# Scores on half-row operands, values with high and low parts side by side, and an earlier copy of the values' difference, in a windowed-attention layer

## The reference, cut to what matters

```python
def sliding_window_attention(u, wqkv, gq, gk, sinks, wo):
    ...
    q = rmsnorm(q, gq)
    k = rmsnorm(k, gk)
    ...
    scores = jnp.einsum('bnqkgd,bnskd->bnkgqs', qb, kb).astype(jnp.float32) * (HD ** -0.5)
    ...
    scores = scores - slopes[:, :, None, None] * dist.astype(jnp.float32)
    scores = jnp.where(mask[None, :, None, None], scores, -jnp.inf)
    sink = sinks.astype(jnp.float32).reshape(KV, G)[:, :, None]
    m = jnp.maximum(scores.max(axis=-1), sink)
    e = jnp.exp(scores - m[..., None])
    probs = e / (e.sum(axis=-1) + jnp.exp(sink - m))[..., None]
    o = jnp.einsum('bnkgqs,bnskd->bnqkgd', probs.astype(v.dtype), vb)
    return o.reshape(b, s, H * HD) @ wo
```

## Time and profile before

| | us |
|---|---|
| median of 3 runs | 1116.42 (1115.62 to 1116.71) |
| profiled execution | 1118.16 |
| its span | 1116.4 |
| the two attention stages and what lies around them | about 0 to 300 |
| MLP and embedding | about 300 to 1116 |

### The profile page before, as it was taken

One profiled execution on the slowest core, in us unless ns is written; L12 is line 12 of the kernel. 1 busy time (PEld: TensorE's weight loads), 2 busy tenths in 40 slices (PEclk: granted clock), 3 DMA queues, 4 the chain that ended last, 5 costly groups with the idle time before them and its releaser, 6 DMA issues.

```text
span 1116.4 us, 14894 instructions
## 1 busy us (share of the span) xinstructions
PE 1089.0 (98%) x5272; PEld 913.1 (82%) x5272; DVE 735.2 (66%) x1130; ACT 428.2 (38%) x776; POOL 148.9 (13%) x272
## 2 busy tenths in 40 slices
PE   7899999998999999999999999999999999999998
PEld 5788888887888888888888888888888888888886
DVE  6677776777544499876677667498777863664311
ACT  7456555565423233313322343453333331243100
POOL 6543444443100000000000000000000000010000
PEclk9999999998999999999999999999999999999999
DMA  7000000121152407343353244998888872111210
GB/s 264 20 20 19 19 1 19 38 111 79 38 170 80 147 1 256 139 171 132 119 201 139 88 188 164 396 411 297 293 287 294 282 250 76 38 38 57 88 45 38
DMA packets 61361, 153.88 MB, mean 138 GB/s; under 512 B 4720, under 2 KB 5752, under 8 KB 61304
## 3 DMA queue, kind: packets, MB, share of 16 engines
q1 hardware_dynamic: 61280, 153.12, 38.4%
q10 hardware_dynamic: 24, 0.01, 0.0%
HBM read 119.03 MB, written 34.08 MB: 137 GB/s over the span
## 4 chain that ended last, share of the span: by engine, by line
PE 81%; DVE 8%; issue 4%; ACT 3%; POOL 2%; ACTq 0%; DVEq 0%; POOLq 0%
PE pair L2204 24%; PE pair L2184 21%; PE pair L2056 8%; PE pair L2247 8%; PE pair L1919 6%; PE pair L2224 4%; PE pair L2142 3%; PE pair L1990 2%; PE pair L2260 2%; ACT probs L938 2%; PE pair L2112 1%; PE pair L1958 1%; DVE probs L1387 1%; ACT kn L891 1%; POOL k_rstd L693 1%
## 5 line engine op out<-in xcount | busy, mean ns | idle before, releaser
L2204 PE MATMUL pair<-uT 128*128 128x512 f32 x1176 | 266.7, 389 | 0.0
L2204 PEld LDWEIGHTS pair<-uT 128*128 128x128 f32 x1176 | 220.7, 188 | 45.8
L1919 PE MATMUL pair<-WA,xT 128*128 128x512 f32 x384 | 97.4, 403 | 11.8 <-DVE kn L1326 7.8
L1193 ACT ACTIVATE uT<-wo_raw 128x1024 fp32r<-128x1024 f32 x63 | 64.3, 1055 | 105.7 <-PE pair L2204 92.7
L1735 DVE TENSOR_TENSOR uT<-wo_raw,uT 128x1024 fp32r<-128x1024 f32 x63 | 75.0, 1222 | 39.3 <-ACT uT L1193 39.2
L675 POOL TENSOR_SCALAR row_var<-row_ssq 128x1 f32<-128x1 f32 x16 | 3.1, 193 | 700.3 <-ACT hn L1092 700.3
L1919 PEld LDWEIGHTS pair<-WA,xT 128*128 128x128 f32 x384 | 70.7, 191 | 29.3 <-issue 13.2
L2056 PE MATMUL pair<-WA,oT 128*128 128x512 f32 x384 | 91.8, 397 | 2.6 <-DVE WA L1491 2.1
L2056 PEld LDWEIGHTS pair<-WA,oT 128*128 128x128 f32 x384 | 72.2, 191 | 17.8 <-issue 3.1
L2184 PE MATMUL pair<-WA,WB 128*128 128x512 f32 x336 | 78.2, 389 | 0.4 <-ACT xr L1168 0.4
L2184 PEld LDWEIGHTS pair<-WA,WB 128*128 128x128 f32 x336 | 63.0, 188 | 13.8 <-DVE WB L1669 0.8
(11 more groups left out here) (203 smaller groups left out, 1877.9 us busy)
## 6 DMA issues: line engine op xcount, KB each, us to landing
wo_raw<-in_m_w SPq DMA_DIRECT2D x53, 512.0 KB, 6.5
wo_raw<-hid_kept SPq DMA_DIRECT2D x36, 512.0 KB, 4.7
hid_kept<-RES SPq DMA_DIRECT2D x28, 512.0 KB, 2.6
emb<-in_m_w SPq DMA_DIRECT2D x20, 512.0 KB, 6.2
RES<-in_m_w SPq DMA_DIRECT2D x8, 1024.0 KB, 6.8
uT_f<-in_m_w SPq DMA_DIRECT2D x6, 1024.0 KB, 6.7
act_buf<-hid_kept SPq DMA_DIRECT2D x11, 512.0 KB, 4.9
hn<-in_m_w SPq DMA_DIRECT2D x11, 512.0 KB, 5.9
```

What stands on the lines that cost most here:

```text
L1193: nc.scalar.activation(operand(t, which, HI), unit(t, which), ACT.Copy).then_inc(op_hi, 1)
L1919: mm = nc.tensor.matmul(proj_bank[X][:], xT[:, s, kt, :], w[:, m, kt, at:at + BANK], start=(kt == 0 and i == 0), stop=(kt == KT - 1 and i ...
L2204: mm = nc.tensor.matmul(ps[4 * (j % 2) + m][:], operand(t, 0, s)[:, k, m * P:(m + 1) * P], operand(t, 1, r)[:, k, :], start=(g == 0 and k ...
```

## The change

**Scores.** `qT` now has its high parts in one half and its low parts in another, each with the even head of a pair in rows 0 to 63 and the odd head in rows 64 to 127. A matmul takes 64 rows of both operands, so a head needs all three passes: 12 matmuls of 256 columns per group instead of 8. Even heads write bank 2 and odd heads bank 3, in turn. `scores_ready` is signalled once per group. The masked copy of `add_bias` is one instruction for four heads instead of two for two heads each, and the high and low parts of q are one 128-row instruction each instead of two of 64 rows.

**Values.** `vz` has for each head its high and its low part side by side (64 + 64 columns), with no zeros. One matmul multiplies both with the probabilities of all four heads: 4 matmuls of 512 columns per group. High products land in PSUM rows 0 to 63, low ones in rows 64 to 127. ACT copies the high rows to `RES` in two instructions (even, odd heads) and signals `pv_copied`; then DVE adds the low rows in two instructions (`add_lows`), and these signal `attended`.

**Copy.** In `body` on GpSimd, `dv_hi_part(n)` stands ahead of `head_norm("q0", n + 1)`. The code of block 0 keeps its order. The clearing of `vz` (L695) is gone.

```diff
@@ -144,10 +144,11 @@
         xT = sb("xT", [P, 2, KT, P], F32R, in_a)
         kn = sb("kn", [P, 2 * KV * HD], F32, in_a)
         qn = sb("qn", [P, H * HD], F32, in_a)
-        qT = sb("qT", [P, H, P], F32R, in_a)
+        qT = sb("qT", [P, 2, H // 2, P], F32R, in_a)
         kT = sb("kT", [P, 2, KV, 2, P], F32R, in_a)
         vnext = sb("vnext", [P, KV * HD], F32, in_a)
-        vz = sb("vz", [P, 2, 2, (2 * KV + 1) * HD], F32R, in_a)
+        vz = sb("vz", [P, 2, KV, 2, HD], F32R, in_a)
+        sb("after_vz", [P, 1280], F32, in_a)
         pT = sb("pT", [P, 2, 2, BANK], F32R, in_a)
         probs = sb("probs", [P, 2, G, P + 2], F32, in_a)
         vprev = sb("vprev", [P, KV * HD], F32, in_a)
...
@@ -778,9 +774,9 @@
                 if not last:
                     x_norm(n + 1)
                 place_sinks(n, 2)
+                dv_hi_part(n)
                 if not last:
                     head_norm("q0", n + 1)
-                dv_hi_part(n)
                 mask_probs(4 * n)
                 if not last:
                     keep_v(n)
...
@@ -920,13 +911,12 @@
                 nc.scalar.activation(kT[:, HI, :, 1, :], ps[6][:].rearrange("p (a n) -> p a n", a=KV),
                                      ACT.Copy, scale=gk_col).then_inc(T_hi["k"], 1)
 
-            def q_hi_part(X, b, odd):
+            def q_hi_part(X, b):
                 act.wait_ge(turned[X], b + 1)
 
-                wait(act, scores_ready, 8 * b + (-4 if X == "q0" else 0))
-                rows = q_rows(odd, HI)
-                nc.scalar.activation(qT[rows, q_heads(X, odd), :], turn_bank[X][rows, :].rearrange("p (a n) -> p a n", a=G),
-                                     ACT.Copy, scale=gq_s[rows, :]).then_inc(T_hi[X], 1)
+                wait(act, scores_ready, 4 * b + (-2 if X == "q0" else 0))
+                nc.scalar.activation(qT[:, HI, q_pairs(X), :], turn_bank[X].rearrange("p (a n) -> p a n", a=G),
+                                     ACT.Copy, scale=gq_s[:]).then_inc(T_hi[X], 1)
 
             def exps(n, j):
                 t, i = 4 * n + j, j % 2
@@ -951,8 +941,10 @@
 
                 act.wait_ge(w_split, U_W1)
                 act.wait_ge(pv_done, t + 1)
+
                 dst = RES[:].rearrange("p b n -> p (b n)")[:, bass.ds(n * D + j * 2 * P, 2 * P)]
-                nc.scalar.activation(dst, pv_bank[:, 0:2 * P], ACT.Copy).then_inc(attended, 1)
+                nc.scalar.activation(dst[0:HD, :], pv_bank[0:HD, 0:2 * P], ACT.Copy)
+                nc.scalar.activation(dst[HD:P, :], pv_bank[0:HD, 2 * P:4 * P], ACT.Copy).then_inc(pv_copied, 1)
 
             def before(n, j, lag):
 
...
@@ -1337,43 +1325,49 @@
                     scalar=gk_col, in1=kT[:, HI, :, 1, :].bitcast(F32), op0=ALU.mult,
                     op1=ALU.subtract).then_inc(T_ready["k"], 1)
 
-            def q_lo_part(X, b, odd):
-
-                high, low = q_rows(odd, HI), q_rows(odd, LO)
-                dve.wait_ge(T_hi[X], 2 * b + (1 + odd))
+            def q_lo_part(X, b):
+                dve.wait_ge(T_hi[X], b + 1)
                 nc.vector.scalar_tensor_tensor(
-                    out=qT[low, q_heads(X, odd), :], in0=turn_bank[X][high, :].rearrange("p (a n) -> p a n", a=G),
-                    scalar=gq_s[high, :], in1=qT[high, q_heads(X, odd), :].bitcast(F32), op0=ALU.mult,
+                    out=qT[:, LO, q_pairs(X), :], in0=turn_bank[X].rearrange("p (a n) -> p a n", a=G),
+                    scalar=gq_s[:], in1=qT[:, HI, q_pairs(X), :].bitcast(F32), op0=ALU.mult,
                     op1=ALU.subtract).then_inc(T_ready[X], 1)
+
+            def add_lows(n, j):
+
+                dve.wait_ge(pv_copied, 4 * n + (j + 1))
+                dst = RES[:].rearrange("p b n -> p (b n)")[:, bass.ds(n * D + j * 2 * P, 2 * P)]
+                nc.vector.tensor_tensor(dst[0:HD, :], pv_bank[HD:P, 0:2 * P], dst[0:HD, :], ALU.add)
+                nc.vector.tensor_tensor(dst[HD:P, :], pv_bank[HD:P, 2 * P:4 * P], dst[HD:P, :],
+                                        ALU.add).then_inc(attended, 1)
+
+            def before(n, j, lag):
+                return (n, j - lag) if j >= lag else (n - 1, j - lag + GROUPS)
 
             def v_diff(b):
                 dve.wait_ge(v_staged, b + 1)
                 if isinstance(b, int) and b == 0:
-                    dve.wait_ge(zeros_ready, 3)
+                    dve.wait_ge(zeros_ready, 2)
                 wait(dve, dv_moved, 2 * b)
                 nc.vector.tensor_tensor(vprev[:], vprev[:], vnext[:], ALU.subtract).then_inc(v_diffed, 1)
 
             def v_lo_part(b):
-                def values(slot, s):
-                    return vz[:, slot, s, HD:(2 * KV + 1) * HD].rearrange("p (v a d) -> p v a d", v=KV, a=2)[:, :, 0, :]
                 dve.wait_ge(v_hi, b + 1)
-                nc.vector.tensor_tensor(values(1, LO), vnext[:].rearrange("p (v d) -> p v d", v=KV),
-                                        values(1, HI).bitcast(F32), ALU.subtract).then_inc(v_ready, 1)
+                nc.vector.tensor_tensor(vz[:, 1, :, LO, :], vnext[:].rearrange("p (v d) -> p v d", v=KV),
+                                        vz[:, 1, :, HI, :].bitcast(F32), ALU.subtract).then_inc(v_ready, 1)
                 dve.wait_ge(dv_moved, 2 * b + 1)
-                nc.vector.tensor_tensor(values(0, LO), vprev[:].rearrange("p (v d) -> p v d", v=KV),
-                                        values(0, HI).bitcast(F32), ALU.subtract).then_inc(v_ready, 1)
+                nc.vector.tensor_tensor(vz[:, 0, :, LO, :], vprev[:].rearrange("p (v d) -> p v d", v=KV),
+                                        vz[:, 0, :, HI, :].bitcast(F32), ALU.subtract).then_inc(v_ready, 1)
 
             def add_bias(n, j, first):
 
                 t, i = 4 * n + j, j % 2
                 if first:
                     dve.wait_ge(current_ready, 2)
-                for half_bank in range(2):
-
-                    stand(dve, scores_ready, 2 * t + (1 + half_bank))
-                    nc.vector.copy_predicated(score_keys[half_bank][:, :, 0, :],
-                                              current[:].bitcast(U32).unsqueeze(1).to_broadcast([P, 2, P]),
-                                              score_keys[half_bank][:, :, 1, :]).then_inc(wrapped, 1)
+
+                stand(dve, scores_ready, t + 1)
+                nc.vector.copy_predicated(score_keys[:, :, 0, :],
+                                          current[:].bitcast(U32).unsqueeze(1).to_broadcast([P, G, P]),
+                                          score_keys[:, :, 1, :]).then_inc(wrapped, 1)
                 for r in range(G):
                     if r == 0:
                         if first:
...
@@ -1420,22 +1413,25 @@
                     wo_lo_unit(1)
                     pT_lo_part(t - 1, (j - 1) % 2)
                     v_diff(n)
+                    add_lows(n - 1, 2)
...
@@ -1479,6 +1473,8 @@
                         k_lo_part(n + 1)
                     if not (first and j < 1):
                         pT_lo_part(t - 1, (j - 1) % 2)
+                    if not (first and j < 2):
+                        add_lows(*before(n, j, 2))
                     if j == 0:
                         v_diff(n)
                     if j == 1:
...
@@ -1568,6 +1564,7 @@
                 h_norm(b - 1, b - 1, 2)
 
             add_attention(0, False)
+            add_lows(NB - 1, 3)
             oT_lo_half(2, 0)
             oT_lo_half(2, 1)
             h_norm(0, 0, 2)
...
@@ -1948,17 +1945,20 @@
 
 
                 t = 4 * n + j
-                pe.wait_ge(T_ready["q0" if j < 2 else "q8"], 2 * n + 2)
+                pe.wait_ge(T_ready["q0" if j < 2 else "q8"], n + 1)
                 pe.wait_ge(T_ready["k"], n + 1)
 
                 wait(pe, biased, 4 * t)
-                for r in range(G):
-                    dst = score_bank[r // 2][:, (r % 2) * 2 * P:(r % 2 + 1) * 2 * P]
-                    for m in (HI, LO):
-                        mm = nc.tensor.matmul(dst, qT[:, G * j + r, :], kT[:, m, j, :, :].rearrange("p a n -> p (a n)"),
-                                              start=(m == HI), stop=(m == LO))
-                    if r % 2 == 1:
-                        mm.then_inc(scores_ready, 1)
+
+                for a in range(2):
+                    for i, (s, m) in enumerate(PASSES):
+                        for odd in range(2):
+                            rows = slice(odd * HD, (odd + 1) * HD)
+                            mm = nc.tensor.matmul(score_bank[odd][:, a * 2 * P:(a + 1) * 2 * P],
+                                                  qT[rows, s, G // 2 * j + a, :],
+                                                  kT[rows, m, j, :, :].rearrange("p a n -> p (a n)"),
+                                                  start=(i == 0), stop=(i == 2))
+                mm.then_inc(scores_ready, 1)
 
             def turn_probs(n, j):
                 t = 4 * n + j
@@ -1984,13 +1984,11 @@
                     if kt == 0:
                         pe.wait_ge(pT_masked, 2 * t + 2)
```

(12 more changed lines are left out.)

76 lines of the change are left out of this document (32 added, 44 removed).

## The result

The changed kernel took **1130.93 us** (median of 5 runs, 1128.45 to 1132.19) against 1116.42 for the kernel before (5 runs, 1115.00 to 1117.53). The ratio is 1.0129, 95% interval 1.0114 to 1.0144: 14.5 us slower, where 11 us faster was forecast. The profiled execution has a span of 1127.7 against 1116.4.

The account below looks back on a forecast made before the run. TensorE, busy 98% of the span, was taken as the bound, with VectorE, ScalarE and GpSimd limiting what its savings bring. -0.2 + 9.0 + 1.7 = 10.5, plus 0.5, made 11 us less: 1105.5, range 1097 to 1111.

Parts of the forecast that it names:

- Values on TensorE: The values' matmuls of each group: 0.91 us instead of 1.42 or 1.51, saving some 0.56 per group.
- Scores on TensorE: The scores' matmuls of each group: twelve on half rows make 1.05 us against 1.03, taken as no change.
- array empties: Rival, chance 0.07: changing operand height around each group's scores costs 0.31 us per group on TensorE; kernel 1108 to 1112.
- VectorE and ScalarE: Work per block: `add_lows` 0.7 us per group, merged masked copy nothing, fewer q parts; net +1.3 on VectorE.
- T to S: From the start of the values after projection q0 to projection q8: 1.3 us shorter, a wait of about 1.2 stays.
- S to the next Q: From the start of projection q8 to the next projection q0: 0.2 us shorter, bounds -1.1 and +0.6.
- Q to T: From the start of projection q0 to the values after it: all matmuls, change 0.
- The block: One block of the attention loop, 31.44 us before: 1.5 us shorter, 9.0 over blocks 1 to 6.
- The clock: Rival, chance 0.05: more idle time lowers TensorE's clock, costing 11 us in seven blocks; 1116.9, no change.
- Block 0: The first attention block: 1.7 us faster (0.6 to 3.3), 0.6 from values and 1.1 from the chain.
- Block 7: The last attention block, with VectorE in the way: 0.2 us slower, -2 to +2.
- slower case: Rival, chance 0.08: half-row score matmuls don't overlap at all, 0.282 us each, 3.4 per group; kernel 1162.

Follow-up runs that it names:

- copy_early_alone: The kernel before with only GpSimd's copy of the values' difference moved ahead of the queries' inverse root: 1110.06 us, ratio 0.9936.
- lows_moved_half_rows: The changed kernel with two masked copies, the values' low rows copied to SBUF by ScalarE and added by GpSimd in one instruction: 1117.50 us.

## Why the prediction was wrong, by its own steps

**Values on TensorE: right.** 0.91 as forecast in two groups (143.17 less 142.26) and 1.01 or 1.02 in the other two, 0.5 less per group in each, where some 0.56 was forecast.

**Scores on TensorE: nearly right.** Taken as no change; 0.11 per group more. Pairs do overlap (0.91 for twelve), and the change of operand height costs 0.29. The "array empties" rival had the mechanism and, at 0.31, nearly its price of 0.29, but it did not count that pairs side by side give 0.13 back (0.16 net by these rows, 0.11 by the blocks). It is not what made the kernel slower.

**VectorE and ScalarE: the step that failed.** `add_lows` was priced at 0.7 per group "from start to start" from a 128x256 row. That price held for neighbours that start at the same row. The row meant for the half-row width (64x512 against 128x512) compares durations and could not show a late start; the pair costs 1.02. The merged masked copy was priced at nothing by its duration, which was right (0.70), but its reader must wait for the result with no other work in between: 0.2 to 0.3 more per group. So a row that TensorE already waited for got 1.2 to 1.3 us longer in each group instead of 0.7. ScalarE's second copy, 0.37, also stands ahead of the probabilities' high part, for which VectorE waits 0.28 and 0.36 in two groups of a block at full clock (`<-ACT pT L937`), where it waited 0.8 and nothing before. Net on VectorE the sum was +1.3 per block; the windows show 2.1 (24.98 against 22.89).

**T to S: forecast -1.3, measured +0.2** (T 142.26, S 155.42: 13.16 against 12.97). The 1.24 of GpSimd's copy did go, as forecast, but with 1.02 of `add_lows` in its place the masked copy of group 2 gained 0.08 after T, and the 0.28 of the merged copy behind it makes that the +0.2. The 0.7 that the single q high was to give gave nothing: q's high part and group 1's exponentials were later on the clock of T, since group 1's masked copy now starts at T - 2.27 (139.99) instead of T - 3.90 (135.38). So the chain was late already on entry, and the late entry is the next step. Two smaller terms of this part were off as well. By its own rows TensorE would have been ready at T + 10.8 and not T + 10.4 (12.97 less the wait of 1.15 and two times 0.51), a wait of 0.9 instead of 1.2. And the early copy was worth more than its 1.24 in copy_early_alone, where the masked copy of group 2 starts 1.75 earlier after T, in part because the values' second low part there lasts 0.42 instead of 0.83; in the changed kernel it lasts 0.85.

**S to the next Q: forecast -0.2, measured +1.0** at full clock (189.19 to 202.71 is 13.52, against 12.51). The prediction let pauses take the 0.65 that it found over. The real surplus was 2.04 for two `add_lows` and 0.5 for two merged copies, less one q low of 0.75: 1.8. Pauses took 0.8 of it. Already the bias of group 3 starts 2.20 after S (157.62) and not 1.19 (153.44 after 152.25). The bound of +0.6 that the prediction gave was for its own surplus, and fell with it.

**Q to T: forecast 0, measured +0.1** (6.05).

**The block: forecast -1.5, measured +1.3** at full clock. Six times that is 7.8; three blocks with a lowered clock add 3.1, and one such stretch in the kernel before, which is gone, takes 1.6 off: 9.3, where 9.2 was measured.

**The clock: a rival at 0.05 that came about in part.** It spoke of idle time in waits close together. After 1.01 to 1.20 and 1.15 us of wait the granted clock fell in three blocks of the six (18 matmuls in 5.96 instead of 4.35), at 0.95 in the mean of such a block, and once more ahead of block 7 after 0.80 and 1.03. In the other three blocks, with waits of 0.97 to 1.03 and 1.03 to 1.14, it stayed full, so these rows don't tell when it falls. Filling the waits gave 4 us back.

**Block 0: right in sign** (-1.2 for -1.7). **Block 7: forecast +0.2, measured +3.3.** 1.6 of it is the clock at its start, as above, which the forecast of this block left out. In the rest, the thing that "would make the whole wrong" did happen, once: the values wait 1.60 for `add_lows`, and the scores and the split output weights come later (the last of these waits was 2.06 before):

```profile
266.27 1.16 PE L1989 MATMUL pair<-pT,vz 128*128 128x512 f32 x4 [1.60 <-DVE RES L1340]
...
277.37 0.98 PE L1957 MATMUL pair<-kT,qT 64*128 64x256 f32 x12 [1.82 <-DVE rmax L1380]
281.42 2.90 PE L2054 MATMUL pair<-WA,oT 128*128 128x512 f32 x6 [3.08 <-DVE WA L1487]
```

**The rivals.** The one slower case was built on TensorE, half rows that don't overlap. The case that happened had the same sign for another reason, and the prediction had all its parts in hand: a chain that TensorE waits for, and work added to it in every group against one piece taken away in one. It took the chain's gains at full size and priced its additions by the cheapest row, and no rival asked what happens when the surplus on VectorE is twice as large.

## What to carry to other kernels

When TensorE waits for another engine even once per block, cost a change on that engine's row first, instruction by instruction from start to start, with the start rows of each operand beside those of its neighbours; what TensorE saves counts only up to where that row lets it. Gains that lie in the same place of one row don't add: build each part alone and then in pairs. Merging two instructions can lose time if the next one reads the result, since the second of them was filling the wait for the first.

## What the runs showed of the hardware that I had not expected

- On VectorE, an instruction that starts at another row (64 after 0, or back) than the one before in that memory starts 0.1 us later: 0.33 becomes 0.42 to 0.46, and 0.60 becomes 0.72.
- A VectorE instruction that waits for the result of the one just ahead starts 0.29 to 0.30 after that one's end in three groups and 0.17 after it in group 0 (L1380 behind L1368).
- A VectorE subtraction of 128x256 in SBUF that starts right behind the start of a GpSimd mask lasts 0.83 to 0.85 instead of 0.42; if it starts 0.10 ahead of the mask it lasts 0.41, and the mask 0.81 instead of 0.64. The cause was not tested.
- Two matmuls of 256 columns on different halves of the rows and in different banks run side by side: twelve in 0.91, 0.076 each, against 0.129 for one on all rows. Entering costs 0.18 behind the transposes and leaving 0.11 ahead of projection k; in group 0 it is 0.09 and 0.05.
- Matmuls without use in TensorE's waits, eight per block, made the kernel after 4.2 us faster and lows_moved_half_rows 2.0.
